# A decoder's third FFN ends with tokens on the partitions, and mixer B's attention begins in another order

## The reference

```python
m = jax.nn.sigmoid(g_a) * (attn_o @ w_pa) + jax.nn.sigmoid(g_f) * (four_o @ w_pf)
y = m @ w_out
x = x + gt1 * rmsnorm_2(y, g_post1)
h2 = modulate(rmsnorm_2(x, g_pre2), sh2, sc2)
u, gate = jnp.split(h2 @ w_up, 2, axis=-1)       # 2 x 2816 channels, then a 3-tap convolution on u
x = x + gt2 * rmsnorm_2((jax.nn.silu(u) * gate) @ w_down, g_post2)
```

## Time and profile before

| | |
|---|---|
| median of 3 runs | 2167.69 us (2163.6 to 2168.49) |
| the profiled execution, its own time | 2167.15 us |
| its span | 2165.4 us |
| PE busy, share of the span | 92% |
| DVE, ACT, POOL busy | 52%, 31%, 40% |

### The profile page before, as it was taken

How to read it: one execution, slowest core, us unless ns; L and a number is a source line. 1 busy time by engine, 2 the same in 40 slices (tenths; PEclk the granted TensorE clock), 3 DMA queues, 4 the chain that set the end, 5 groups by cost and what they waited for, 6 DMA issues and landing times.

```text
span 2165.4 us, 25929 instructions
## 1 busy us (share of the span) xinstructions
PE 2001.3 (92%) x9702; PEld 1598.4 (74%) x9702; DVE 1122.4 (52%) x2007; ACT 670.7 (31%) x1058; POOL 871.2 (40%) x648
## 2 busy tenths in 40 slices
PE   3989789999999988989999999999999959999997
PEld 3766467788778776558788887788876848888886
DVE  7777874533943675754534534872233554312334
ACT  3233463321122124562321222234444222212211
POOL 4343103444744552105445544542221423444442
PEclk9999899999999999999999999999999979999998
DMA  4222001422532341003324422332110212223221
GB/s 159 78 79 97 25 1 63 165 98 73 209 136 91 139 150 59 25 23 110 117 91 149 160 97 104 104 105 76 59 59 20 98 57 79 85 80 117 97 80 66
DMA packets 32205, 199.14 MB, mean 92 GB/s; under 512 B 3696, under 2 KB 3824, under 8 KB 14320
## 3 DMA queue, kind: packets, MB, share of 16 engines
q1 hardware_dynamic: 27216, 166.74, 22.0%
q10 hardware_dynamic: 4896, 31.15, 4.0%
HBM read 195.78 MB, written 2.10 MB: 91 GB/s over the span
## 4 chain that ended last, share of the span: by engine, by line
PE 49%; DVE 4%; ACT 1%; POOL 1%; issue 1%; DVEq 0%; ACTq 0%
PE psum L1514 42%; PE psum L1536 2%; PE psum L1707 2%; PE psum L1689 1%; POOL w_lo L565 1%; PE psum L1672 1%; PE psum L1974 1%; DVE xT L1024 1%; DVE work L1018 1%; PE psum L1644 0%; ACT w_hi L595 0%; PE psum L1635 0%; DVE work L1029 0%; DVE h_lo L1008 0%; PE psum L1628 0%
## 5 line engine op out<-in xcount | busy, mean ns | idle before, releaser
L565 POOL TENSOR_TENSOR w_lo<-raw,w_hi 128x512 fp32r<-128x512 f32 (+2 forms) x640 | 862.7, 1376 | 1264.8 <-ACT w_hi L595 1264.8
L1514 PE MATMUL psum<-h_hi,w_hi 128*128 128x512 f32 x1560 | 614.2, 394 | 14.1 <-POOL w_lo L565 6.6
L1514 PE MATMUL psum<-h_hi,w_lo 128*128 128x512 f32 x1560 | 611.2, 392 | 0.0
L1514 PE MATMUL psum<-h_lo,w_hi 128*128 128x512 f32 x1560 | 610.5, 391 | 0.0
L595 ACT ACTIVATE w_hi<-raw 128x2048 fp32r<-128x2048 f32 (+3 forms) x177 | 301.6, 1704 | 565.7 <-PE psum L1514 474.4
L1514 PEld LDWEIGHTS psum<-h_hi,w_hi 128*128 128x128 f32 x1560 | 294.0, 188 | 87.4 <-issue 14.5
L1514 PEld LDWEIGHTS psum<-h_hi,w_lo 128*128 128x128 f32 x1560 | 293.7, 188 | 63.6 <-issue 2.4
L1514 PEld LDWEIGHTS psum<-h_lo,w_hi 128*128 128x128 f32 x1560 | 293.8, 188 | 62.2 <-issue 2.3
L1514 PE MATMUL psum<-g_hi,w_hi 128*128 128x512 f32 x528 | 207.6, 393 | 10.9 <-POOL w_lo L565 5.8
L1514 PE MATMUL psum<-g_hi,w_lo 128*128 128x512 f32 x528 | 205.6, 389 | 0.0
L1514 PE MATMUL psum<-g_lo,w_hi 128*128 128x512 f32 x528 | 205.6, 389 | 0.0
(11 more groups left out here) (312 smaller groups left out, 2424.1 us busy)
## 6 DMA issues: line engine op xcount, KB each, us to landing
raw<-w_up SPq DMA_DIRECT2D x66, 1024.0 KB, 4.8
raw<-w_dn SPq DMA_DIRECT2D x48, 704.0 KB, 4.1
mod_w<-w_mod ACTq DMA_DIRECT2D x24, 1024.0 KB, 4.9
raw<-w_c_in SPq DMA_DIRECT2D x13, 1024.0 KB, 4.9
raw<-w_b_in SPq DMA_DIRECT2D x7, 1024.0 KB, 4.9
raw<-w_a_idx SPq DMA_DIRECT2D x5, 1024.0 KB, 5.7
raw<-w_a_out SPq DMA_DIRECT2D x8, 640.0 KB, 3.9
raw<-w_b_out SPq DMA_DIRECT2D x8, 640.0 KB, 3.9
```

The costliest lines, as they stand in the source:

```text
L565: ins = nc.gpsimd.tensor_tensor(LO[slot][:, a:z], RAW[slot][:, a:z], HI[slot][:, a:z].bitcast(F32), ALU.subtract)
L1514: ins = nc.tensor.matmul(out, l, r, start=(k == 0 and m == 0), stop=(k == n - 1 and m == 2))
```

## The change

**Mixer B.** The units of `b_in` come as keys, first queries, values. PE no longer waits for the values' copies and waits for three of the four turned tiles ahead of `attend`; 12 products of the remaining units are done ahead of the first transposes (`AHEAD_B`), then 6 a step. ACT loads its Exp table during `b_in`. In the steps, `rope` is cut in two (`later`): shuffle and cosine product now, sine product and sum one step later.

**The norm pre2** sums by narrow products into banks 0 to 3, and root and reciprocal work on 128x4. Between them PE turns the residual `XT` (32 transposes of 128x128, `turned_rows`), and ACT copies it to `XROWS`, tokens on the partitions (`rows_copy`).

**The third FFN's down projection** has tokens on the partitions: the stationary operand is a 128-token tile of g, the moving one 512 columns of weights. For each half h and each half f of the output channels there are two units of four chunks and one of three, each used by all four token tiles t. The gates of `post2` are laid out once as rows (`GATE`). In the last part (h=1, f=1) the second and third unit are worked token tile by token tile; the squares of a token are then summed along the row by ACT itself, and each tile is gated, scaled, added to `XROWS` and stored by SP in two halves while PE works on the next.

```diff
-          ("b_in", 7, 2048, [2, 4, 2, 2, 2, 2, 2]), ("b_out", 8, 1280, 1),
+          ("b_in", 7, 2048, [2, 2, 4, 2, 2, 2, 2]), ("b_out", 8, 1280, 1),
...
-          ("up20", HALF, 2048, 2), ("dn20", 8, HALF * P, 1), ("up21", HALF, 2048, 2), ("dn21", 8, HALF * P, 1)]
+          ("up20", HALF, 2048, 2), ("dn200", 2, 2048, 1), ("dn201", 1, 1536, 4), ("dn202", 2, 2048, 1), ("dn203", 1, 1536, 4),
+          ("up21", HALF, 2048, 2), ("dn210", 2, 2048, 1), ("dn211", 1, 1536, 4), ("dn212", 2, 2048, 1), ("dn213", 1, 1536, 4)]
...
-        FILL_MEM, FILL_B, FILL_C, LAST_C = 12, 7, 40, 12
+        FILL_MEM, FILL_B, AHEAD_B, FILL_C, LAST_C = 12, 6, 12, 40, 12
+
+        def b_finished(k):
+
+            return (AHEAD_B + FILL_B * k) // 24 if k > 0 else 0
...
-                if u == 1:
+                if u == 0:
+                    nc.scalar.activation(WARM[:, 14:15], cst("eps"), ACT.Exp)
+                if u == 2:
                     for t in range(ROWT):
-                        act.wait_ge(ph.done, ph.before(1) + t + 1)
+                        act.wait_ge(ph.done, ph.before(2) + t + 1)
                         nc.scalar.activation(BV[:, t, :], bank(4 + t, 0, 256), ACT.Copy).then_inc(qkv_ready, 1)
             hi_split(ph.split + 4)
...
+            def rows_copy(k):
+                act.wait_ge(x_turned, k + 1)
+                nc.scalar.activation(XROWS[:, :, k * P:(k + 1) * P], bank(6 + k % 2).rearrange("p (t n) -> p t n", t=ROWT),
+                                     ACT.Copy).then_inc(x_rows, 1)
+
+            def beside_squares(k):
+                if k in (3, 4, 7):
+                    rows_copy({3: 0, 4: 1, 7: 2}[k])
+
+            def beside_pre2(k):
+                if k < 3:
+                    rows_copy(3 + k)
+
+                 beside=beside_pre2, with_squares=beside_squares, shift=lambda k: MODV[:, 24 + k, 0:1])
+            rows_copy(6)
+            rows_copy(7)
+            for h in range(2):
+                ffn_up(PH[f"up2{h}"], 44 + h * HALF)
+                if h == 1:
+                    nc.scalar.activation(WARM[:, 13:14], cst("eps"), ACT.Sqrt)
+                for n in range(4):
+                    stream_only(PH[f"dn2{h}{n}"])
+                    if h == 1 and n == 1:
+                        for t in range(ROWT):
+                            act.wait_ge(rows_read, 8 + t + 1)
+                            nc.scalar.activation(T[:, t, :], Y2[:, t, 0:S], ACT.Square,
+                                                 accum_out=YSUM[:, 0, t:t + 1]).then_inc(y_squared, 1)
+            act.wait_ge(y_biased, 1)
+            for t in range(ROWT):
+                act.wait_ge(rows_read, 12 + t + 1)
+                nc.scalar.activation(T[:, t, :], Y2[:, t, S:D], ACT.Square, accum_out=YSUM[:, 1, t:t + 1]).then_inc(y_squared, 1)
+                act.wait_ge(y_squared, 4 + t + 1)
+                nc.scalar.activation(ROOT[:, t:t + 1], YSUM[:, 1, t:t + 1], ACT.Sqrt, bias=YBIAS[:, t:t + 1],
+                                     scale=1.0 / D).then_inc(y_root, 1)
...
+                if later:
+                    step(nc.vector.tensor_tensor(dst, src, cos[0:n, :], ALU.mult))
+
+                    def rest():
+                        step(nc.vector.tensor_tensor(sw, sw, sin[0:n, :], ALU.mult))
+                        nc.vector.tensor_tensor(dst, dst, sw, ALU.add).then_inc(done, 1)
+                    return rest
...
             for c in range(2):
-                b_tile(2, c, BQ[:, c, :], c + 3)
             def b_between(k):
-                for tile in range(min(finished(FILL_B, k - 1) if k else 0, 6), min(finished(FILL_B, k), 6)):
-                    b_tile(3 + tile // 2, tile % 2, BQ[:, 2 + tile, :], 5 + tile)
+                if begun:
+                    begun.pop()()
+                for tile in range(min(b_finished(k - 1), 6), min(b_finished(k), 6)):
+                    begun.append(b_tile(3 + tile // 2, tile % 2, BQ[:, 2 + tile, :], 5 + tile, later=True))
...
-            ffn(2, Y2, ("copy", "add"))
-            norm("post2", lambda k: Y2[:, k, :], lambda k: DER[:, 4, k:k + 1], into="x")
...
+                ffn_up(PH[f"up2{h}"], 2, h, (4 + h) * HALF, [(PH["dn203"].done, ROWT)] if h else [])
+                if h == 0:
+                    v.wait_ge(gate_laid, 1)
+                    for half in range(2):
+                        nc.vector.tensor_copy(GATE[:, half * S:(half + 1) * S], bank(6 + half)).then_inc(gate_ready, 1)
+                for f in range(2):
+                    if h == 1 and f == 1:
+                        v.wait_ge(gate_ready, 2)
+                        v.wait_ge(rows_read, 12)
+                        for t in range(ROWT):
+                            step(nc.vector.tensor_tensor(YG[:, t, 0:S], Y2[:, t, 0:S], GATE[:, 0:S], ALU.mult))
+                        v.wait_ge(y_squared, ROWT)
+                        nc.vector.tensor_scalar(YBIAS[:], YSUM[:, 0, :], 1.0 / D, EPS, ALU.mult, ALU.add).then_inc(y_biased, 1)
+                    for t in range(ROWT):
+                        rows = Y2[:, t, f * S:(f + 1) * S]
+                        v.wait_ge(PH[f"dn2{h}{2 * f + 1}"].done, t + 1)
+                        if h == 0:
+                            nc.vector.tensor_copy(rows, bank(4 * f + t)).then_inc(rows_read, 1)
+                            continue
+                        nc.vector.tensor_tensor(rows, bank(4 * f + t), rows, ALU.add).then_inc(rows_read, 1)
+                        if f == 0:
+                            continue
+                        v.wait_ge(rows_read, 12 + t + 1)
+                        step(nc.vector.tensor_tensor(YG[:, t, S:D], rows, GATE[:, S:D], ALU.mult))
+                        v.wait_ge(y_root, t + 1)
+                        step(nc.vector.reciprocal(INV[:, t:t + 1], ROOT[:, t:t + 1]))
+                        for half in range(2):
+                            part = slice(half * S, (half + 1) * S)
+                            nc.vector.scalar_tensor_tensor(out=XROWS[:, t, part], in0=YG[:, t, part], scalar=INV[:, t:t + 1],
+                                                           in1=XROWS[:, t, part], op0=ALU.mult, op1=ALU.add).then_inc(out_ready, 1)
...
+                    for t in range(ROWT):
+                        bank_free(t)
+                    for k in range(nch):
+                        pe.wait_ge(square_ready, b + k + 1)
+                        for t in range(ROWT):
+                            ins = nc.tensor.matmul(bank(t, 0, 1), T[:, k % 2, t * P:(t + 1) * P], ONES[:, 0:1],
+                                                   start=k == 0, stop=k == nch - 1)
+                        ins.then_inc(square_used, 1)
+                        if k >= 1:
+                            advance(turning, 2)
+                    advance(turning, 4)
+                    bank_free(5)
+                    pe.wait_ge(pre2_inverse, 1)
+                    for t in range(ROWT):
+                        ins = nc.tensor.matmul(bank(5, t * P, (t + 1) * P), INV[:, t:t + 1].broadcast_to([P, P]),
+                                               cst("ident", P), start=True, stop=True)
+                    ins.then_inc(pre2_spread, 1)
+                    advance(turning, 8)
...
-                if u == 1:
-                    last_read[4] = (scaled_ready, NORMS["mix1"][4] + DC)
+                if u == 2:
                     advance(r_tiles(ph, u, range(4), range(4, 8), 0, 256))
...
-                    if k % 4 == 2 and 2 <= group < 8:
+                    if k == 0:
+                        advance(rest, AHEAD_B)
+                    if k % 4 == 2 and group < 8:
                         pe.wait_ge(ph.free, 3 + group)
-                    elif k % 4 == 2 and group == 8:
-                        pe.wait_ge(qkv_ready, 15)
+                    elif k % 4 == 2 and group < 10:
+                        pe.wait_ge(qkv_ready, 6 + group)
                 else:
                     advance(rest, FILL_B)
-            pe.wait_ge(qkv_ready, 13)
-            pe.wait_ge(ph.free, 4)
+            pe.wait_ge(ph.free, 3)
...
-            norm("pre2")
-            ffn(2, "pre2")
-            norm("post2")
+
+            def turned_rows():
+                for k in range(DC):
+                    bank_free(6 + k % 2)
+                    pe.wait_ge(x_ready, XR["post1"] + k + 1)
+                    for t in range(ROWT):
+                        ins = nc.tensor.transpose(bank(6 + k % 2, t * P, (t + 1) * P), XT[:, k, t * P:(t + 1) * P], cst("ident", P))
+                        if t == ROWT - 1:
+                            ins.then_inc(x_turned, 1)
+                            last_read[6 + k % 2] = (x_rows, k + 1)
+                        yield
+            turning = turned_rows()
+            norm("pre2", turning=turning)
+
+            def gate_rows(u):
+                if u == 0:
+                    advance(turning)
+                if u != 1:
+                    return
+                for k in range(DC):
+                    if k % 4 == 0:
```

(47 more changed lines are left out.)

75 lines of the change are left out of this document (51 added, 24 removed).

## The result

The changed kernel takes 2152.34 us (median of 4, 2151.65 to 2153.0) against 2167.03 (median of 4, 2163.6 to 2168.49) for the kernel before: ratio 0.9933, 95% interval 0.9917 to 0.9949. It is faster, but by 14.7 us where I had said 23.9, and it lies just above my range of 2134 to 2152. The two profiled spans, 2165.4 and 2151.2, differ by 14.2, so the traces show the gain to be explained.

What follows compares the result with a forecast made beforehand. PE bounds the kernel, busy 2001.3 of 2165.4 us, so only its idle time at three seams can be won. 7.5 + 5.5 + 3.6 - 2.6 + 9.9 = 23.9 off 2167.15 gives 2143.2 us; range 2134 to 2152.

Steps and rivals of the forecast that it cites:

- The steps: Mixer B's attention: cut rope and longer filling remove 5.5 of 9.8 us of PE's waits; bounds 0 and 9.8.
- the slow half: Rope's sine product and sum, both reading two SBUF operands; under POOL the sum takes 1.66 us against 0.69 for the cosine product.
- The start: Start of mixer B's attention: first transposes 3.6 us earlier, more from the clock; 7.5 us gained, bounds 3.6 and 9.
- the 1.5 that I had set as a sign: Start of mixer B's attention: PE has no idle stretch over 1.5 us between 827 and the first transposes.
- The 2.6 us for the clock: Start of mixer B's attention: the 5.3 us behind 835.52 take half that at granted clock 1.00, 2.6 us more gained.
- the third rival: Mixer B gives little: waits stay, moved by a step, start gains only 3.6; 9.4 us less gain, 2152.6; chance 0.12.
- pre2: Norm pre2: sums need not wait for `post1`, clock stays 0.50, `up20` starts 3.6 us earlier; bounds 2.0 and 11.7.
- The first rival: Norm pre2: PE keeps up as the clock is granted during the sums; `up20` 8.1 us earlier than forecast, 2135.1; chance 0.17.
- Added to PE's path: In `up20`: six transposes behind its first unit, gates' 16 instructions behind its second; 2.6 us lost, bounds 2 and 3.6.
- the fourth rival: Down projection: swapped roles cost PE 0.045 us more per product, 0.272 in place of 0.227, so slower than before; chance 0.03.
- The end: Behind the last product 6.1 us in place of 19.25, less a PE wait of 3.2: 9.9 gained, bounds 8.5 and 10.5.

Runs made afterwards that it cites:

- pool_none_before: Kernel before, with POOL splitting only 16 of 2048 columns of mixer B's units from the fourth on (low parts stale): 2153.7 us, ratio 0.9941.
- whole_rope: Changed kernel with each of the six ropes in the attention's filling whole in one step again, all else as changed: 2155.89 us, ratio 0.9954.
- split_late: Changed kernel with ACT's split of mixer B's fifth unit issued behind the first attention step's exponentials, no longer ahead of them: 2152.44 us, ratio 0.9936.
- tail_two: Changed kernel; in the down projection's last quarter PE does the second unit for two token tiles, not one, ahead of the third unit: 2146.3 us, ratio 0.9902.
- pool_fine: Changed kernel with POOL splitting mixer B's units from the fourth on in pieces of 256 columns in place of 512: 2141.46 us, ratio 0.9882.
- pool_128: Changed kernel with POOL splitting mixer B's units from the fourth on in pieces of 128 columns in place of 512: 2140.99 us, ratio 0.9886.

## Why the prediction was wrong

**The steps: the wrong step.** "What is late then is the scaling of that step" was right; its cause was not. I saw POOL slow a sum and a scaling and priced it by the rope, as a slow half that could be halved. In the wait shown above it is DVE's L1164 and its two scalings that are late beside POOL's split, with no rope instruction among them. The steps' waits were 9.8 us and are 9.5 (11.2 less the 1.72 ahead of the first transposes), so the term of 5.5 was worth 0.3. `pool_none_before` shows that 6.2 of the 10.8 were POOL's from the start. I also had the filling wrong: I took the new order and filling for a help, and by `whole_rope` they cost 3.2 us of waiting, which eats up the 3.5 of the cut. My doubt that the cut would put the slow half under POOL was also off: none of the six halves ran beside POOL.

**The start: right mechanism, size off.** The gap of 3.99 us went and PE's 12 products filled it. The first transposes came at 833.13, not at 831.9, 2.4 earlier than before in place of 3.6: I had let the first scaling take 1.0 and it took 2.27 beside POOL. The wait of 1.72 us is also over the 1.5 that I had set as a sign. The 2.6 us for the clock did not come: the low stretch of 10.2 us at 830.55 became one of 3.4 at 833.90, but another of 3.4 followed each of the two waits of 3.49, where the kernel before had one (at 868.10), and PE's busy time in the stretch stayed at 159.1. `split_late` shows the start alone could have had 1.8 more and that the steps would have taken it back. Start and steps together gave 4.3 in place of 13.0, 4.1 of it ahead of the attention. This is the third rival, "mixer B gives little": 2152.6 by its working, 2152.34 measured; 0.12 was too low for it. So close a match is luck in part: its reason, the slow half, was not the cause, and smaller misses cancel: mixer B gave 0.7 and pre2 0.9 us more than that sum has, the stretch up to `c_out` 0.6 and the down projection 1.4 less. The rule of the Trainium skill that I weighed ("GPSIMD Engine Reference", 1. Specifications) fits as a mechanism, but showed nothing against the cut, since no second half met POOL; what it spoke against was the attention beside POOL's split, in both kernels.

**pre2: right.** 4.5 for 3.6. The clock stayed at 0.50 through all sums and the pace was 2.03 us a chunk (1.71 for the sums), where I had 2.2; the wait of 1.3 behind a copy measured 1.20. The first rival, sums at pace, did not happen.

**Added to PE's path: right**, 2.6. The 264 products of the first half took 60.10 us, 0.228 each: swapped roles cost nothing, and the fourth rival is out.

**The end: right but for the clock.** From DVE's first instruction behind the last product to the end it took 5.9 for 6.1, and the wait 2.72 for 3.2. I left out the low clock behind the wait, 1.6 us, as `tail_two` shows. 8.7 in place of 9.9.

**Left open:** the 0.6 us lost between mixer B and `c_out`. A stretch of low clock at 1407.34 that the kernel before doesn't have lies there, opposite a wait of 0.99 that went; no run took it apart.

## What to carry to other kernels

When DVE is late beside POOL, find out first whether its instructions end where POOL's do: if so, try shorter POOL instructions (0.5% of this kernel for one changed loop bound) before lightening DVE. Price a wait of PE together with a low clock that may follow: the wait of 2.72 us in the last quarter cost 4.3 with it. And compare a stretch only where the clock at its start is the same, or cut it behind that start. A filling that is moved into a gap can't remove waits that belong to something else; take the suspected cause out for one run before pricing it.

## What the runs showed of the hardware that was not expected

An addition of two elements per partition on DVE took 1.25 us while POOL ran subtractions of 512 columns (1.26 each), and 0.42 at pieces of 128. POOL's cost per instruction: 5.03 us for a unit in 4, 6.57 in 8, 7.73 in 16, disturbed by DVE in all three. PE's granted clock fell to 0.50 for 3.4 us behind the waits of 1.72, 3.49 and 3.49 us in the changed kernel's attention and the one of 2.72 in the last quarter, and not once in the attention of `pool_fine` and `pool_128`, with up to 9 waits of at most 1.34. It doesn't follow every such wait: the one of 3.24 us that ends at 896.96 in the kernel before, and the one of 1.73 that ends at 829.23 in `whole_rope`, had none behind them. One of PE's instructions with a single moving column (the profile has two for each product) took 0.215 us at 0.50 (13.79 for 64).
